# Two stacked mixers: block 1's feed-forward on rows without the norm's inverse

## The chip, the cores and the metric

One core of a Trainium2 chip runs the whole program. The metric is the device time of one execution in microseconds (us), the median of several runs.

## The reference

A first block of two layers and a second block of two layers run one after the other on the same 256 rows of 1024 values. The change is in the first block's second half, in both of its layers:

```
x = x + rms_norm(m, norm_mix_post[layer])          # m: output of the mixer
h = rms_norm(x, norm_ffn_pre[layer])
f = (silu(h @ w_gate) * (h @ w_up)) @ w_down       # 1024 -> 2816 -> 1024
x = x + rms_norm(f, norm_ffn_post[layer])

def rms_norm(x, w):
    return x * rsqrt(mean(x * x, -1) + 1e-6) * w
```

The norm's inverse root is one number for each token, so it can be applied to h or to the products of h.

## The kernel before

**Layout.** Activations lie with the features on the 128 partitions (eight tiles, k = 0 to 7) and the 256 tokens in the free dimension; xs holds x. Weights come from HBM as one stream of units of eight 128x128 blocks. One unit is one tile of 128 output columns in most products with 1024 rows. SyncE loads a unit into one of three raw buffers (L916), ScalarE rounds it to its high part w_hi (L1514), GpSimd computes the low part w_lo as the difference (L956, two instructions a unit); both are fp32r and have four slots. A raw buffer is free when the low part is done, a slot when TensorE has used the unit. Activations are split in high and low parts in the same way (hl). A product takes three partial products: in product_halves (L1014, L1018) one matmul of 512 columns multiplies the high weights with both halves of hl, one of 256 columns the low weights with the high half, and VectorE adds the two halves of the bank (add_halves, L2004).

**Order.** Every engine runs an order written out by hand, and waits on semaphores that count. Nothing reorders it. SyncE's loads are one list, weights and modulation units by the place of their use. The modulation units belong to block 2: its modulation vectors are computed in gaps of block 1, four fp32 matmuls a unit (modulation_unit, L1165), at named places; MID1 has six and PRE1 two. Behind some gates the finished rows are copied by VectorE (take_modulation, L2112, COPY zrow) and turned by TensorE (turn_modulation, L1176).

**The stretch.** After the output projection TensorE sums the squares of its result over the features, token by token (last_rows_sum, L1101), ScalarE takes the root, VectorE the reciprocal (L1966), and TensorE spreads the inverse over the partitions of a bank (spread_inverse, L1114). VectorE then forms the update (L2073) and adds it to xs (L2077), tile by tile; ScalarE squares the new tile (L1548); TensorE sums these squares (norm_sums), with the MID1 units between. A second root, reciprocal and spread follow, the PRE1 units run, and norm1 makes the rows: VectorE multiplies by weight and inverse (L1975), ScalarE rounds (L1579), VectorE subtracts (L1979). The first gate and up tiles run side by side on each k as it is ready (side_by_side, L1058 to L1061), the other 21 pairs tile by tile. VectorE adds the halves of gate and up, ScalarE applies SiLU (L1625) and rounds the hidden tile (L1770), VectorE multiplies (L2326) and makes the low part (L2320). The tiles ffg and ffu (gate, up) take banks 0, 1 and 3 in turn; bank 2 is STAT, bank 7 is X[4].

Of the kernel before, what the change touches and what calls it, by code (L numbers as in the profile page):

```python
# [12 lines left out]
P = 128  # L13
D = 1024
KD = D // P
# [459 lines left out]
SINGLE1, SINGLE2 = 1, 3  # L475


class Place:


    def __init__(self):
# [3 lines left out]
        for t in TILES:  # L485
            self.first_out.append(out)
            self.first_block.append(block)
            n = 1
            if t.wide == 2:
                n = 2 if t.array == "w_in" else T2 // P  # L490
            self.outs.append(n)
            pool = MANY if t.name in ("fa", "fg", "fd") or t.array == "w_out_2" else FEW
            if t.name in ("fa", "fg", "fd") and t.layer == DEPTH - 1:
                pool = THREE
            if t.array == "w_in" and t.name not in ("rg", "gr", "gate"):
                pool = WITH_STAT
            if t.array == "w_in_2" and t.name in ("ca", "cg"):
                pool = THREE
            if t.name in ("ffg", "ffu") or t.array in ("w_branch_a", "w_branch_b", "w_branch_c") or (t.array, t.name) == ("w_in", "gate"):
                pool = THREE  # L500
            for i in range(out, out + n):
                at = pool[(pool.index(self.bank[-1]) + 1) % len(pool)] if i and self.bank[-1] in pool else pool[0]
                self.bank.append(at)
# [54 lines left out]
def mixer_stack_kernel(nc, stream, vectors, consts, decay, gla_masks, positions, x_in, ctx_in, out):  # L558
# [201 lines left out]
    half_sum = STAT[:, 0:SEQ]  # L760


    def sem(name):
# [61 lines left out]
    merge_used, sum_ready, gate1_ready, ffg_ready = [  # L825
        sem(n) for n in ("merge_used", "sum_ready", "gate1_ready", "ffg_ready")]
# [74 lines left out]
    with nc.Block() as block:  # L901
# [66 lines left out]
        def _(pe):  # L968
# [149 lines left out]
            def last_rows_sum(c0, c1, single):  # L1118
# [7 lines left out]
                last.then_inc(stat_ready, 1)  # L1126
                spread_inverse(STAT, c0, c1)

# [59 lines left out]
            for l in range(DEPTH):  # L1188
# [312 lines left out]
        def _(act):  # L1501
# [118 lines left out]
            def on_sum(rows, func, scale, done):  # L1620
# [3 lines left out]
                act.wait_ge(tile_out, n + 1)  # L1624
# [18 lines left out]
            for l in range(DEPTH):  # L1643
# [119 lines left out]
                for t in range(NFF + 1):  # L1763
                    if t < NFF:
                        on_sum(ff_g[:, t % 2, :], ACT.Silu, 1.0, ffg_ready)
                        next_tile()
                        E.later(tile_done, 1)
                    if t:
                        E.need(ff_rows)
                        nc.scalar.activation(hid_hi[:, t - 1, :], half_sum, ACT.Copy).then_inc(ff_hi, 1)  # L1770
# [181 lines left out]
        def _(dve):  # L1952
# [98 lines left out]

            def add_normed(name, l):
# [17 lines left out]
                written = []  # L2070
                for k in range(KD + 1):
# [62 lines left out]
            for l in range(DEPTH):  # L2134
# [178 lines left out]
                dve.wait_ge(x_ready, KD * (2 * l + 1))  # L2313
                norm1("norm_ffn_pre", l)
                for t in range(NFF + 1):
                    if t < NFF:
                        add_halves(ff_g[:, t % 2, :])
# [3 lines left out]
                    if t < NFF:  # L2321
                        if t:
                            dve.wait_ge(ff_ready, NFF * l + t)
                        dve.wait_ge(tile_out, add_halves(half_sum))
                        E.need(ffg_ready)
# [355 lines left out]
```

## Time and profile before

| | us |
|---|---|
| median of 3 runs | 2690.48 (2689.98 to 2695.3) |
| the profiled execution's own time | 2693.33 |
| span of the profile | 2691.4 |
| granted TensorE clock, mean | 0.999 |
| busy: TensorE | 98% |
| busy: GpSimd, VectorE, ScalarE | 60%, 50%, 48% |
| median of the runs below the profiled execution's time | 2.85 |

The profile is of one execution, which took 2.85 us more than the median; its span is the part from the first to the last instruction. A share of busy time is a mean over stages; what the change touches is read from the stretch itself.

### The profile page before, as it was taken

The page shows a single profiled execution, that of the slowest core. Times are in us where ns is not written, and L with a number is a line of the kernel's source. Part 1 is how long each engine was busy: PE and PEld are TensorE (multiplying, and loading weights), DVE is VectorE, ACT ScalarE, POOL GpSimd, SP SyncE. Part 2 cuts the span into 40 slices and gives each one's busy share as a digit, 9 for nine tenths or more (in the row PEclk, how much of TensorE's full clock was granted, in tenths as well). Part 3 has the DMA queues.
Part 4 walks back from the last instruction along what each step waited for, and adds up shares of the span by engine and source line. Part 5 has one row for each costly group of instructions (what it writes and reads, how often), then busy time and mean ns, then how long its engine had stood idle before and what let it go on. Part 6 is the DMA issues. An engine that isn't in the chain of part 4 may idle for free.

```text
span 2691.4 us, 41592 instructions
## 1 busy us (share of the span) xinstructions
PE 2636.3 (98%) x16130; PEld 2260.6 (84%) x16130; DVE 1357.9 (50%) x2437; ACT 1283.0 (48%) x2042; POOL 1622.5 (60%) x1252
## 2 busy tenths in 40 slices
PE   8999999999999999999999999999999999999999
PEld 7998788899887888786788888888888889999888
DVE  6885533268654344875532434431333855335644
ACT  6464544455544454446433433442343565445654
POOL 6778688778786785432333345344443635458787
PEclk9999999999999999999999999999999999999999
DMA  6458676444787743221112122223222423234454
GB/s 216 141 182 283 228 255 226 160 139 154 253 274 236 248 167 124 84 74 56 63 63 87 63 88 101 87 94 102 94 94 79 142 86 118 95 110 157 166 187 165
DMA packets 145011, 386.12 MB, mean 143 GB/s; under 512 B 11968, under 2 KB 64448, under 8 KB 144832
## 3 DMA queue, kind: packets, MB, share of 16 engines
q1 hardware_dynamic: 144832, 383.61, 42.1%
q8 instruction: 128, 2.10, 0.3%
q14 instruction: 51, 0.42, 0.1%
HBM read 382.51 MB, written 1.05 MB: 143 GB/s over the span
## 4 chain that ended last, share of the span: by engine, by line
POOL 49%; issue 44%; PE 6%; POOLq 1%; DMA 0%; DVE 0%; ACT 0%; DVEq 0%; ACTq 0%
POOL w_lo L956 49%; PE bank L1014 4%; PE bank L1018 2%; POOLq L953 0%; DMA raw<-stream 0%; POOLq L960 0%; PE bank L1000 0%; PE bank L999 0%; PE bank L998 0%; ACT w_hi L1514 0%; DVE bank L2624 0%; ACT fc L1936 0%; DVE fc L2631 0%; DVE bank L2643 0%; POOLq L956 0%
## 5 line engine op out<-in xcount | busy, mean ns | idle before, releaser
L956 POOL TENSOR_TENSOR w_lo<-raw,w_hi 128x512 fp32r<-128x512 f32 x1248 | 1622.3, 1330 | 1060.4 <-ACT w_hi L1514 1057.7
L1514 ACT ACTIVATE w_hi<-raw 128x1024 fp32r<-128x1024 f32 x624 | 656.0, 1055 | 390.2 <-DMA raw<-stream 167.4
L998 PE MATMUL bank<-hl,w_hi 128*128 128x256 f32 (+1 forms) x2000 | 682.7, 341 | 1.9 <-POOL w_lo L956 1.0
L1000 PE MATMUL bank<-hl,w_lo 128*128 128x256 f32 (+1 forms) x2000 | 668.4, 334 | 0.0
L999 PE MATMUL bank<-hl,w_hi 128*128 128x256 f32 (+1 forms) x2000 | 668.3, 334 | 0.0
L998 PEld LDWEIGHTS bank<-hl,w_hi 128*128 128x128 f32 x2000 | 380.0, 190 | 45.7 <-issue 6.6
L999 PEld LDWEIGHTS bank<-hl,w_hi 128*128 128x128 f32 x2000 | 380.1, 190 | 41.0 <-issue 3.6
L1000 PEld LDWEIGHTS bank<-hl,w_lo 128*128 128x128 f32 x2000 | 379.8, 190 | 37.9
L1014 PE MATMUL bank<-hl,w_hi 128*128 128x512 f32 x1296 | 339.4, 395 | 2.8 <-POOL w_lo L956 2.5
L1014 PEld LDWEIGHTS bank<-hl,w_hi 128*128 128x128 f32 x1296 | 231.8, 189 | 50.4 <-issue 9.0
L1018 PEld LDWEIGHTS bank<-hl,w_lo 128*128 128x128 f32 x1296 | 178.9, 190 | 13.1
L1018 PE MATMUL bank<-hl,w_lo 128*128 128x256 f32 x1296 | 183.0, 282 | 0.0
L2631 DVE SCALAR_TENSOR_TENSOR fc<-bank,vec,fc 128x510 f32<-128x510 f32 (+1 forms) x88 | 54.2, 616 | 178.4 <-ACT fc L1936 178.4
L2361 DVE SCALAR_TENSOR_TENSOR xs<-bank,mod,xs 128x256 f32<-128x256 f32 x93 | 42.7, 481 | 177.5 <-PE bank L1000 132.8
L1014 PE MATMUL bank<-hid,w_hi 128*128 128x512 f32 x462 | 126.9, 394 | 0.0
L1936 ACT ACTIVATE fc<-bank,vec 128x512 f32<-128x512 f32 (+1 forms) x88 | 59.1, 672 | 141.9 <-PE bank L1000 108.8
L2416 DVE SCALAR_TENSOR_TENSOR bank<-z,vec,bank 128x512 f32<-128x512 f32 (+1 forms) x232 | 123.1, 617 | 0.0
L998 PE MATMUL bank<-y,w_hi 128*128 128x256 f32 (+1 forms) x336 | 110.6, 329 | 5.1 <-ACT gate L1537 4.4
L1081 PE MATMUL bank<-w_hi,hl 128*128 128x256 f32 x384 | 111.0, 289 | 2.0 <-POOL w_lo L956 1.4
L1000 PE MATMUL bank<-y,w_lo 128*128 128x256 f32 (+1 forms) x336 | 108.7, 324 | 0.0
L999 PE MATMUL bank<-y,w_hi 128*128 128x256 f32 (+1 forms) x336 | 108.6, 323 | 0.0
L1082 PE MATMUL bank<-w_lo,hl 128*128 128x256 f32 x384 | 108.6, 283 | 0.0
(330 smaller groups left out, 4066.4 us busy)
## 6 DMA issues: line engine op xcount, KB each, us to landing
raw<-stream SPq DMA_DIRECT2D x624, 512.0 KB, 3.3
spare_lo<-stream SPq DMA_DIRECT2D x32, 512.0 KB, 6.1
mix<-stream SPq DMA_DIRECT2D x32, 512.0 KB, 6.1
spare_hi<-stream SPq DMA_DIRECT2D x32, 512.0 KB, 5.8
xs<-x_rows SPq DMA_DIRECT2D x4, 256.0 KB, 4.1
xs<-ctx_rows SPq DMA_DIRECT2D x1, 1024.0 KB, 13.4
out_rows<-xs SPq DMA_DIRECT2D x8, 128.0 KB, 3.4
dec<-decay SPq DMA_DIRECT2D x1, 768.0 KB, 10.4
```

Source lines behind the costliest of these rows:

```text
L956: last = nc.gpsimd.tensor_tensor(w_lo[:, unit % SPLIT, part], raw[:, unit % RAW, part], w_hi[:, unit % SPLIT, part], ALU.subtract)
L998: nc.tensor.matmul(acc, wh, x[:, 0, k, c0:c1], start=k == 0, stop=False)
L999: nc.tensor.matmul(acc, wh, x[:, 1, k, c0:c1], start=False, stop=False)
L1000: last = nc.tensor.matmul(acc, wl, x[:, 0, k, c0:c1], start=False, stop=k == t.k - 1)
L1014: return nc.tensor.matmul(acc[:, :], w, x[:, :, k, c0:c1], start=k == 0, stop=k == t.k - 1)
L1018: return nc.tensor.matmul(acc[:, 0:SEQ], w, x[:, 0, k, c0:c1], start=False, stop=False)
L1081: nc.tensor.matmul(acc, h_hi[:, k, c:c + P], wh, start=k == 0, stop=False)
L1082: nc.tensor.matmul(acc, h_hi[:, k, c:c + P], wl, start=False, stop=False)
L1514: nc.scalar.activation(w_hi[:, n % SPLIT, :], raw[:, n % RAW, :], ACT.Copy).then_inc(hi_ready, 1)
L1936: nc.scalar.activation(fc[:, t % 2, j, cols], rows, ACT.Identity, bias=v_("ffn_conv_b_2", l, i), scale=v_("ffn_conv_w_2", l, 2 * NFF + i)) ...
L2416: C.do(V.scalar_tensor_tensor(out, z, w, y, MUL, ADD))
L2631: C.do(V.scalar_tensor_tensor(y[:, :, 1:], u[:, :, 0:SEQ - 1], w[0], y[:, :, 1:], MUL, ADD))
```

## The change

The rows of the feed-forward no longer contain the inverse: h is x times the weight, and every sum of the gate and up tiles is multiplied by the inverse, token by token, from a copy in sd, before SiLU or the product (add_scaled for the gate, a tensor_tensor for up). The sum of squares, the root and the spread of that inverse therefore run behind the first three tiles (gate, up, gate) instead of ahead of them: rows_before_norm takes each k of three tiles and then the sums of that k. The fourth tile gets a bank of its own, 5. One MID1 unit goes between the first sum and its spread, five follow the spread; the PRE1 units stand between the second sum and its spread. VectorE forms the update in bank 5, so that the addition to xs has one operand in PSUM. ScalarE makes the high part straight from xs with the weight as its scale, and rounds the fourth weight unit ahead of these rows, two more behind the second root, the others behind the first SiLU and the first hidden tile. The high part of a hidden tile now goes ahead of the next SiLU.

```diff
+    def update_row(k):
+        return banks[RAW_BANK][:, k % 2 * SEQ:(k % 2 + 1) * SEQ]
...
@@ TensorE
-                last_rows_sum(c0, c1, SINGLE1)
-                norm_sums(c0, c1, X[4], ADA_AT[l][MID1])
+                mid = ADA_AT[l][MID1]
+                last_rows_sum(c0, c1, SINGLE1, mid[:1])
+                rows_before_norm(hl, c0, c1, RAW_TILES, X[4], mid[1:])
                 modulation_at(l, PRE1)
-                for t in range(NFF):
-                    if t:
+                spread_inverse(X[4], c0, c1)
+                pe.wait_ge(ada_rows_out, MODS * l + 2)
+                product_halves(hl, c0, c1)
+                modulation_at(l, FFNS[0])
+                for t in range(1, NFF):
+                    if t > 1:
                         product_halves(hl, c0, c1, 2)
-                    else:
-                        side_by_side(hl, c0, c1, 2, h_ready, halves=True)
                     modulation_at(l, FFNS[t])
...
+            def rows_before_norm(x, c0, c1, count, bank, units):
...
+                for k in range(KD):
+                    E.need(h_ready)
+                    for i, acc in enumerate(accs):
...
+                        last = nc.tensor.matmul(acc[:, :], wh, x[:, :, k, c0:c1], start=k == 0, stop=k == KD - 1)
...
+                    E.need(sq_ready)
+                    last = token_sums(bank, work[:, k, :], c0, c1, k == 0, k == KD - 1)
...
@@ ScalarE
-                squares_of_x(c0, c1)
+                split_freed()
+                for k in range(KD):
+                    E.need(x_ready)
+                    nc.scalar.activation(h_hi[:, k, c0:c1], xs[:, k, c0:c1], ACT.Copy,
+                                         scale=v_("norm_ffn_pre", l, k)).then_inc(hi_done, 1)
+                    square(k, xs, c0, c1, sq_ready)
                 token_roots(X[4], c0, c1)
-                split_norm(c0, c1)
...
@@ VectorE
+            def add_scaled(dst):
+                n = E.later(tile_out, 1) - 1
+                dve.wait_ge(tile_done, n + 1)
+                V.reduce_sum(gate_sum, both_halves(banks[PLACE.bank[n]]), AX_X).then_inc(tile_out, 1)
+                dve.wait_ge(tile_out, n + 1)
+                V.tensor_tensor(dst, gate_sum, sd[:, 0:SEQ], MUL).then_inc(ffg_scaled, 1)
...
+                    for k in range(KD + 1):
+                        if k < KD:
+                            C.do(V.scalar_tensor_tensor(update_row(k), mix[:, k, c0:c1], v_(name, l, k),
+                                                        STAT[:, c0:c1], MUL, MUL))
+                        if k:
+                            E.need(hi_done)
+                            V.scalar_tensor_tensor(h_lo[:, k - 1, c0:c1], xs[:, k - 1, c0:c1],
+                                                   v_("norm_ffn_pre", l, k - 1), h_hi[:, k - 1, c0:c1], MUL, SUB)\
+                                .then_inc(h_ready, 1)
+                        if k < KD:
+                            C.settle()
+                            V.tensor_tensor(xs[:, k, c0:c1], update_row(k), xs[:, k, c0:c1], ADD).then_inc(x_ready, 1)
+                    token_inverses(c0, c1)
+                    C.do(V.tensor_copy(sd[:, 0:SEQ], X[4][:, c0:c1]))
...
-                norm1("norm_ffn_pre", l)
                 for t in range(NFF + 1):
-                    if t < NFF:
-                        add_halves(ff_g[:, t % 2, :])
                     if t:
                         dve.wait_ge(ff_hi, NFF * l + t)
                         V.tensor_tensor(hid_lo[:, t - 1, :], half_sum, hid_hi[:, t - 1, :], SUB).then_inc(ff_ready, 1)
                     if t < NFF:
+                        add_scaled(ff_g[:, t % 2, :])
...
                         dve.wait_ge(tile_out, add_halves(half_sum))
+                        C.do(V.tensor_tensor(half_sum, half_sum, sd[:, 0:SEQ], MUL))
+                        C.settle()
                         E.need(ffg_ready)
                         V.tensor_tensor(half_sum, ff_g[:, t % 2, :], half_sum, MUL).then_inc(ff_rows, 1)
```

TensorE in layer 0, from the first sum to the first tiles, before (the numbers ahead of the rows are places in its order; silu_c rows are modulation units, four matmuls each, cst,work rows are sums, cst,sd rows spreads):

```order
1491 L1101 MATMUL bank<-cst,work 128x128 x4
1492 L1114 MATMUL bank<-cst,sd 128x128 x2
1493 L1165 MATMUL bank<-spare_hi,silu_c 2x256 x8
1494 L1165 MATMUL bank<-spare_lo,silu_c 2x256 x4
1495 L1101 MATMUL bank<-cst,work 128x128 x4
1496 L1165 MATMUL bank<-spare_lo,silu_c 2x256 x4
...
1501 L1101 MATMUL bank<-cst,work 128x128 x4
1502 L1114 MATMUL bank<-cst,sd 128x128 x2
1503 L1165 MATMUL bank<-spare_hi,silu_c 2x256 x8
1504 L1059 MATMUL bank<-hl,w_hi 128x512
```

And now, the same place:

```order
1491 L1110 MATMUL bank<-cst,work 128x128 x4
1492 L1201 MATMUL bank<-spare_hi,silu_c 2x256 x4
1493 L1123 MATMUL bank<-cst,sd 128x128 x2
1494 L1201 MATMUL bank<-spare_hi,silu_c 2x256 x4
1495 L1201 MATMUL bank<-spare_lo,silu_c 2x256 x8
1496 L1201 MATMUL bank<-mix,silu_c 2x256 x8
...
1504 L1154 MATMUL bank<-hl,w_lo 128x256
1505 L1155 MATMUL bank<-hl,w_hi 128x512
...
1509 L1155 MATMUL bank<-hl,w_hi 128x512
1510 L1110 MATMUL bank<-cst,work 128x128 x2
```

The sums of the second norm, which stood together between the units, now stand one k at a time behind six matmuls of three tiles.

VectorE at the start of the feed-forward's tiles, before (ff_g is the gate tile's sum, zrow the copy of the modulation rows):

```order
238 L1979 TENSOR_TENSOR hl<-work,hl 128x256 x3
239 L2004 TENSOR_REDUCE ff_g<-bank 128x256
240 L2004 TENSOR_REDUCE bank<-bank 128x256
241 L2326 TENSOR_TENSOR bank<-ff_g,bank 128x256
242 L2112 COPY zrow<-bank 128x256
```

And now:

```order
236 L2022 RECIPROCAL sd<-sd 128x2
237 L2148 COPY sd<-bank 128x256
238 L2111 TENSOR_REDUCE bank<-bank 128x256
239 L2113 TENSOR_TENSOR ff_g<-bank,sd 128x256
240 L2060 TENSOR_REDUCE bank<-bank 128x256
241 L2403 TENSOR_TENSOR bank<-bank,sd 128x256
242 L2406 TENSOR_TENSOR bank<-ff_g,bank 128x256
243 L2192 COPY zrow<-bank 128x256
244 L2396 TENSOR_TENSOR hid<-bank,hid 128x256
```

The copy of the modulation rows stands behind six instructions that wait for the second spread.

## Rows read from the trace of the kernel before

**Rows 1.** The page: busy time of TensorE; the rounding of weights by ScalarE.

```profile
PE 2636.3 (98%) x16130; PEld 2260.6 (84%) x16130; DVE 1357.9 (50%) x2437; ACT 1283.0 (48%) x2042; POOL 1622.5 (60%) x1252
...
L1514 ACT ACTIVATE w_hi<-raw 128x1024 fp32r<-128x1024 f32 x624 | 656.0, 1055 | 390.2 <-DMA raw<-stream 167.4
```

**Rows 2.** Timeline, TensorE, layer 0's stretch and layer 1's start: start, us, engine, instruction.

```profile
305.48 1.35 PE L1101 MATMUL bank<-cst,work 128*128 128x128 f32 x8
...
307.38 0.71 PE L1114 MATMUL bank<-cst,sd 128*128 128x128 f32 x4 [0.55 <-DVE sd L1966]
...
308.02 1.04 PE L1165 MATMUL bank<-spare_hi,silu_c 128*2 128x256 f32 x16
...
308.89 0.61 PE L1165 MATMUL bank<-spare_lo,silu_c 128*2 128x256 f32 x8
...
311.21 0.61 PE L1165 MATMUL bank<-spare_lo,silu_c 128*2 128x256 f32 x8
...
311.76 1.16 PE L1101 MATMUL bank<-cst,work 128*128 128x128 f32 x8
...
312.85 0.61 PE L1165 MATMUL bank<-mix,silu_c 128*2 128x256 f32 x8
...
316.80 0.71 PE L1114 MATMUL bank<-cst,sd 128*128 128x128 f32 x4 [0.62 <-DVE sd L1966]
...
815.22 1.35 PE L1101 MATMUL bank<-cst,work 128*128 128x128 f32 x8
```

**Rows 3.** Timeline, TensorE, first tiles, turned rows, and fp32r behind a unit.

```profile
319.41 0.47 PE L1059 MATMUL bank<-hl,w_hi 128*128 128x512 f32 x1 [0.92 <-DVE hl L1979]
...
325.11 0.40 PE L1014 MATMUL bank<-hl,w_hi 128*128 128x512 f32 x1
...
330.70 0.38 PE L1176 MATMUL bank<-cst,zrow 128*128 128x128 f32 x2
...
330.84 0.48 PE L1014 MATMUL bank<-hl,w_hi 128*128 128x512 f32 x1
...
344.03 0.50 PE L1014 MATMUL bank<-hl,w_hi 128*128 128x512 f32 x1
...
344.37 0.88 PE L1018 MATMUL bank<-hl,w_lo 128*128 128x256 f32 x6
```

**Rows 4.** Timeline, VectorE and ScalarE, the update and the first extraction.

```profile
308.13 0.87 DVE L2073 SCALAR_TENSOR_TENSOR work<-mix,vec,bank 128x256 f32<-128x256 f32 x2 [0.80 <-PE bank L1114]
...
309.26 0.48 DVE L2073 SCALAR_TENSOR_TENSOR work<-mix,vec,bank 128x256 f32<-128x256 f32 x1
...
309.38 0.42 ACT L1548 ACTIVATE work<-xs 128x256 f32<-128x256 f32 x1 [2.24 <-DVE xs L2077]
...
323.88 1.28 ACT L1625 ACT_TABLE_LOAD   x1
...
325.56 0.69 DVE L2004 TENSOR_REDUCE bank<-bank 128x256 f32<-128x512 f32 x1
...
326.28 0.43 DVE L2326 TENSOR_TENSOR bank<-ff_g,bank 128x256 f32<-128x256 f32 x1
...
326.62 0.42 DVE L2112 COPY zrow<-bank 128x256 f32<-128x256 f32 x1
```

**Rows 5.** Lines L2275 and L2320: duration ns min/median/max, first and last start.

```profile
L2275 DVE SCALAR_TENSOR_TENSOR y<-mix,y x16: 411/720/1416, 256.8 to 794.6; 128x256 fp32r<-128x256 f32 x16
...
L2320 DVE TENSOR_TENSOR hid<-bank,hid x44: 424/425/426, 331.1 to 965.2; 128x256 fp32r<-128x256 f32 x44
```

**Rows 6.** Timeline, GpSimd, first unit behind the stretch.

```profile
323.94 2.53 POOL L956 TENSOR_TENSOR w_lo<-raw,w_hi 128x512 fp32r<-128x512 f32 x2 [15.37 <-ACT w_hi L1514]
```

**Rows 7.** Timeline of SyncE; loads from 344 and from 317 us: KB, median us to landing.

```profile
318.12 1.29 SPq L925 DMA_DIRECT2D spare_hi<-stream  x2
...
raw<-stream SPq DMA_DIRECT2D x5, 512.0 KB, 4.8
...
spare_hi<-stream SPq DMA_DIRECT2D x2, 512.0 KB, 7.4
```

More of the change, by code:

```diff
@@ L475 @@
 SINGLE1, SINGLE2 = 1, 3
+RAW_TILES, RAW_BANK = 3, 5
+RAW_LAST = [[t for t in TILES if t.name in ("ffg", "ffu") and t.layer == l][RAW_TILES] for l in range(DEPTH)]
 class Place:
@@ L502, in __init__ @@
                 at = pool[(pool.index(self.bank[-1]) + 1) % len(pool)] if i and self.bank[-1] in pool else pool[0]
+                if t is RAW_LAST[t.layer]:
+                    at = RAW_BANK
                 self.bank.append(at)
@@ L1126, in last_rows_sum @@
                 last.then_inc(stat_ready, 1)
+                for unit in units:
+                    modulation_unit(unit)
                 spread_inverse(STAT, c0, c1)
+            def rows_before_norm(x, c0, c1, count, bank, units):
+                first = at["tile"]
+                accs = [bank_of(PLACE.first_out[first + i]) for i in range(count)]
+                stat_free()
+                for unit in units:
+                    modulation_unit(unit)
+                for k in range(KD):
+                    E.need(h_ready)
+                    for i, acc in enumerate(accs):
+                        u = PLACE.first_block[first + i] // UNIT
+                        wait_unit(u)
+                        wh, wl = w_hi[:, u % SPLIT, k * P:(k + 1) * P], w_lo[:, u % SPLIT, k * P:(k + 1) * P]
+                        if k:
+                            nc.tensor.matmul(acc[:, 0:SEQ], wl, x[:, 0, k, c0:c1], start=False, stop=False)
+                        last = nc.tensor.matmul(acc[:, :], wh, x[:, :, k, c0:c1], start=k == 0, stop=k == KD - 1)
+                        if k == 0:
+                            last = nc.tensor.matmul(acc[:, 0:SEQ], wl, x[:, 0, k, c0:c1], start=False, stop=False)
+                        if k == KD - 1:
+                            last.then_inc(tile_done, 1)
+                    E.need(sq_ready)
+                    last = token_sums(bank, work[:, k, :], c0, c1, k == 0, k == KD - 1)
+                last.then_inc(stat_ready, 1)
+                at["tile"] += count
             def norm_sums(c0, c1, bank, units=(), spread_bank=None, spare=0):
@@ L1618, in square_rows, with on_sum @@
                 nc.scalar.activation(mix[:, KD - 1, c0:c1], last, ACT.Copy).then_inc(tile_out, 1)
-            def on_sum(rows, func, scale, done):
+            def on_sum(rows, func, scale, done, before=None):
                 n = next_tile()
                 E.later(tile_done, 1)
-                act.wait_ge(tile_out, n + 1)
+                if before:
+                    before()
+                    E.need(ffg_scaled)
+                else:
+                    act.wait_ge(tile_out, n + 1)
                 nc.scalar.activation(rows, rows, func, scale=scale).then_inc(done, 1)
@@ L1759, in _, with hidden_high @@
                 token_roots(STAT, c0, c1)
-                squares_of_x(c0, c1)
-                token_roots(X[4], c0, c1)
-                split_norm(c0, c1)
-                for t in range(NFF + 1):
-                    if t < NFF:
[L1765 to L1768, printed above, removed]
-                        E.need(ff_rows)
-                        nc.scalar.activation(hid_hi[:, t - 1, :], half_sum, ACT.Copy).then_inc(ff_hi, 1)
+                split_freed()
[4 more added lines that the diff above has]
+                    square(k, xs, c0, c1, sq_ready)
+                token_roots(X[4], c0, c1)
+                ahead = at["unit"] + 1
+                split_through(ahead)
+                def hidden_high(t):
+                    if t >= 0:
+                        E.need(ff_rows)
+                        nc.scalar.activation(hid_hi[:, t, :], half_sum, ACT.Copy).then_inc(ff_hi, 1)
+                    if t == 0:
+                        split_through(ahead + 2)
+                for t in range(NFF):
+                    on_sum(ff_g[:, t % 2, :], ACT.Silu, 1.0, ffg_ready, lambda: hidden_high(t - 1))
+                    if t == 0:
+                        split_through(ahead + 1)
+                    next_tile()
+                    E.later(tile_done, 1)
+                hidden_high(NFF - 1)
                 square_rows(l == DEPTH - 1)
```

15 lines of the change are left out of this document (9 added, 6 removed).

## The prediction

> **What bounds the kernel now.** I read the page's busy times first: TensorE is busy for 98% of the span [rows 1], so time can be gained only where TensorE stands idle, and work moved off other engines is worth nothing. Then the timeline of TensorE around the place that the diff touches, which is the stretch between block 1's output projection and its feed-forward, once per layer. In layer 0 it begins at 305.48 us (the first matmul of the sum of squares) and reaches the feed-forward's fifth tile, the third gate, at 330.84 [rows 2, 3], 25.36 us later. Layer 1 runs through the same rows from 815.22 [rows 2]. I call 305.48 the origin and count from it.
>
> The reader is to see how full that stretch already is. Its named waits are 0.55 us for the first reciprocal, 0.62 for the second and 0.92 for the first normalised rows [rows 2, 3]. Its work up to the end of the two tiles side by side (325.11, 19.63 us from the origin) is: first sum 1.1, two spreads of 0.64, eight modulation units 4.0, the sums of eight rows 4.4, sixteen pairs of matmuls 5.6, together 16.4 by the prices below. So about 3.2 us per layer are idle, 6.4 in both, 0.24% of the run, and that is the most that the change can bring. In the feed-forward behind it the rows follow one another without a wait.
>
> **The change part by part, for one layer.** All is counted from the origin on TensorE.
>
> *First sum and spread.* The sum is unchanged, 1.35 us with its wait. One modulation unit now stands between it and the spread; two in a row take 0.87 (308.02 to 308.89), a lone one among other matmuls 0.55 (311.21 to 311.76) [rows 2]. It ends at +1.90, and the reciprocal was there before +1.90 too, so the unit is free: spread from +1.92, 0.64 long (307.38 to 308.02), to +2.56. Five units follow: 5 times 0.435 and 0.1 for the switch, 2.28, to +4.84.
>
> *Raw rows, eight steps.* Each step is six matmuls of three tiles and two sums. Sixteen pairs of the two side by side tiles took 5.70 (319.41 to 325.11) [rows 3], 0.35 us each behind the first; three are 1.05. The sums of two steps take 1.09 (311.76 to 312.85), so one 0.545. Together 1.60, or 12.8 us for eight. But the step changes between the two kinds of matmul twice. The first fp32r matmul after fp32 ones holds TensorE 0.34 us (344.03 to 344.37) [rows 3] (a whole pair takes 0.35, and this is its longer half, so some 0.1 of it is the switch), and a lone spread of two matmuls takes 0.64 where two such of a row take 0.545. No row shows this alternation, so its cost is bounded: from 0 to 0.25 a step, and I take 0.17, near the sum of the two differences. Eight steps of 1.77: 14.2 (12.8 to 14.8).
>
> Is TensorE the pace there? The first row needs: spread to VectorE 0.75 (307.38 to 308.13), update 0.48 and add 0.42 (0.43 with a PSUM input), ScalarE 0.42, low part 0.48, and handovers of 0.05 each [rows 2, 4]: +4.6, ahead of +4.84. Each further step is add, ScalarE, low part and handovers, 0.42 + 0.42 + 0.48 + 0.15, about 1.5 (1.3 where the update's issue overlaps), under 1.77. The squares come behind the high part, 0.84 of ScalarE a step, under it too.
>
> *A shared port.* GpSimd now rounds the fourth unit at once, some 308.6 to 311.1, since ScalarE takes it behind the first root (1.05 us [rows 1], while VectorE waits for the spread); in the kernel before, GpSimd stood idle for 15.37 us here [rows 6]. While GpSimd is busy, a VectorE instruction with two SBUF inputs varies: the like of the new low part in the merge took 0.41 to 1.42 us, median 0.72, the one with a PSUM input 0.42 to 0.43 always [rows 5]. The update and its add have a PSUM input; the low part has two SBUF inputs. The first one starts at about +4.1 and may end anywhere from +4.6 to +5.5; I take 0.2 us of TensorE's time, 0 to 0.7. The Trainium skill states in GPSIMD Engine Reference, Key points: GpSimd shares its SBUF interfaces with VectorE and contends with instructions with two SBUF inputs. The trace agrees, with 0.42 against 0.72; by the rule the edit pays up to 0.7 us a layer, without it nothing.
>
> So the eight steps end at 4.84 + 0.2 + 14.2 = +19.24, with three tiles done.
>
> *Second sum, spread and fourth tile.* Two PRE1 units, 0.98, cover the root and the reciprocal (for which TensorE waited 0.62 with nothing between). They end at +20.2. The spread, 0.64, then the fourth tile, eight pairs or 2.80, end at +23.65. In the kernel before the fourth tile ended at about +25.2 (330.70), so the raw rows are worth 1.5 us here.
>
> *A new wait.* Behind the fourth tile TensorE turns the modulation rows (330.70 in [rows 3]), and needs the copy of them by VectorE, which stands behind the first gated product. Before, that copy ran at 326.62, 4 us early [rows 4]. Now all extraction of tiles starts behind the second spread: 0.75 from the spread's start, copy of the inverse 0.42, reduce 0.69, scaling 0.43, reduce 0.69, scaling 0.43, product 0.43, copy of the rows 0.42 [rows 4], less some overlap of issue, with handovers of 0.04: about 4.3 us. From +20.2 that is +24.5, and TensorE, ready at +23.65, waits 0.9 us. The SiLU doesn't add to it: its scaled rows are there 2.4 us after the spread's start, and the table load (1.28) [rows 4], behind the rounding of two units, is over by about 1.8. The two transposes, 0.14, end at +24.7, where the fifth tile starts. Before: +25.36. **Gain 0.66 us per layer.**
>
> *Weights.* At +24.7 units five and six must be rounded. ScalarE starts five 0.3 us after the eight steps, GpSimd takes 2.53 a unit [rows 6]: ready 3.0 us behind the PRE1 units, needed at 4.5. Unit seven's load stands in SyncE's queue behind the eight modulation loads, the last two of which wait for the PRE1 units; it leaves 0.9 us after them (the like two were issued from 318.12 to 319.41) [rows 7]. With modulation loads beside it a weight load landed in 4.8 us, two modulation loads together in 7.4 [rows 7]. With 4.8: 5.7, high part 1.06 [rows 1], low part 2.53, 9.3 us behind the PRE1 units, needed at 10.1 (4.5 and two tiles of 2.80). Hidden by 0.8. Unit eight follows at GpSimd's 2.53 against 2.80.
>
> *Per tile pair* VectorE gets two scalings more, 0.86 us. Its chain in a pair (low part, two reduces, two scalings, product, handovers) is some 3.7 of 5.6 us, and SiLU's lateness of 0.9 leaves the rounding of weights ahead: hidden. At the end the last hidden row is 0.45 later, needed 7.4 us into the down projection: hidden. The fourth tile's own bank keeps it from waiting for the first extraction. TensorE's matmuls are the same in number.
>
> **Sum.** 2 layers of 0.66 are 1.3 us: the profiled execution would have a span of 2690.1 instead of 2691.4, and its own time 2692.0 instead of 2693.3. The median of the runs, 2690.48, lies 2.85 below that time; the same step gives 2689.2. Bounds: with 12.8 for the steps and no contention the gain is 2.2 per layer; with 14.8 and 0.7 it is -0.4.
>
> **Rivals.**
> 1. *Clean interleave*: switching costs nothing. Gain 2.2 per layer, 2686.1. For it: a switch from fp32r to fp32 shows no gap in [rows 3]. Against: the 0.34 us the other way.
> 2. *VectorE and ScalarE set the pace of the eight steps* (slower). Each step is a round trip of three dependent instructions, with two SBUF inputs in one. From 1.85 us a step the gain is gone; at 2.1 a layer loses 2.0, and the time is 2694.5. Against: the parts sum to 1.5.
> 3. *Unit seven late* (slower). If its load behind two modulation loads lands in their 7.4 us, its low part is ready 11.9 behind the PRE1 units against 10.1 needed: 1.9 us per layer lost, net 1.2, the time 2693.0. From 5.6 us of landing on it costs.
> 4. *The change doesn't do what it says*: waits only move (a second wait on the extraction chain), 2690.5.
>
> **How the numbers follow.** The forecast has 0.60, rivals 1 to 4 have 0.12, 0.10, 0.10 and 0.08. Predicted 2689.2. The forecast alone spans 2686.5 to 2691.3; the range 2685.8 to 2693.0 takes in rivals 1, 3 and 4. A measurement of this kernel can tell a change from about 0.2%, 5.4 us. Faster by more needs nearly the whole idle time, 0.04; slower by more needs 2.7 a layer, the tail of rival 2 or 2 and 3 together, 0.07; within it 0.89.
>
> **What would show it.** On TensorE: eight steps of 1.77 us from about 4.9 us after the first sum; the transposes after the fourth tile waiting 0.9 us for VectorE's copy; no wait for a low part at the seventh tile; the fifth tile 24.7 us after the origin. On VectorE low parts of 0.48 but for the first or second. A step over 1.85, with TensorE waiting for VectorE's low part, shows rival 2; a wait for GpSimd at the seventh tile rival 3; steps of 1.6 rival 1. Wrong altogether would be a change of time outside this stretch.

## The result and the profile after

The changed kernel takes 2700.86 us (median of 13 runs, 2696.33 to 2707.41) against 2693.25 for the kernel before (13 runs): ratio 1.0027, with a 95% interval of 1.002 to 1.0035. It is slower by 7.6 us; the prediction had 1.3 us faster and 2693.0 as the upper end of its range. The profiled execution of the changed kernel took 2707.41 us, with a span of 2705.6, 6.5 above its own median. So I compare lengths of stretches within the traces and leave the rest of that execution alone. A second profile of the same kernel (below) took 2701.32.

The stretch runs from the first matmul of the sum of squares to the first matmul of the down projection, once per layer:

| kernel | layer 0, us | layer 1, us |
|---|---|---|
| before | 145.8 | 148.1 |
| after | 149.0 | 153.9 |
| after, second profile | 147.4 | 153.2 |

The second profile is longer by 1.6 and 5.1, together 6.7, where its medians differ by 6.9 (2701.32 against 2694.46). Outside these two stretches the same two traces differ by 1.4 us in sum: single parts by -1.1 to +2.5, and the largest part (from the sum of squares behind layer 1's down projection to the end) takes 1662.5 to 1667.8 us over the fourteen profiles of this text, with no order by kernel. So I look for the loss in the two stretches; the experiments, which take it away there, bear that out. The page after, for [rows 1]:

```profile
PE 2640.9 (98%) x16130; PEld 2265.0 (84%) x16130; DVE 1394.7 (52%) x2511; ACT 1285.8 (48%) x2042; POOL 1619.7 (60%) x1252
```

TensorE has the same 16130 matmul records, yet is busy 4.6 us longer. The timeline of TensorE after (start, us, instruction, idle time before it and what ended it), layer 0 with origin 306.90, then two rows of layer 1; it answers to [rows 2, 3]:

```profile
306.90 1.35 PE L1110 MATMUL bank<-cst,work 128*128 128x128 f32 x8
...
308.80 0.71 PE L1123 MATMUL bank<-cst,sd 128*128 128x128 f32 x4
...
312.55 0.50 PE L1155 MATMUL bank<-hl,w_hi 128*128 128x512 f32 x1 [0.78 <-DVE hl L2141]
...
313.72 0.60 PE L1110 MATMUL bank<-cst,work 128*128 128x128 f32 x4
314.08 0.36 PE L1154 MATMUL bank<-hl,w_lo 128*128 128x256 f32 x1
...
315.22 0.61 PE L1110 MATMUL bank<-cst,work 128*128 128x128 f32 x4
...
324.73 1.05 PE L1201 MATMUL bank<-spare_hi,silu_c 128*2 128x256 f32 x16
325.71 0.71 PE L1123 MATMUL bank<-cst,sd 128*128 128x128 f32 x4
326.18 0.47 PE L1023 MATMUL bank<-hl,w_hi 128*128 128x512 f32 x1
...
330.00 0.44 PE L1212 MATMUL bank<-cst,zrow 128*128 128x128 f32 x2 [0.78 <-DVE zrow L2192]
330.19 0.48 PE L1023 MATMUL bank<-hl,w_hi 128*128 128x512 f32 x1
...
336.76 0.79 PE L1023 MATMUL bank<-hl,w_hi 128*128 128x512 f32 x1 [3.52 <-DVE bank L2111]
337.35 1.91 PE L1027 MATMUL bank<-hl,w_lo 128*128 128x256 f32 x8
339.05 2.49 PE L1023 MATMUL bank<-hl,w_hi 128*128 128x512 f32 x8
...
844.74 0.44 PE L1212 MATMUL bank<-cst,zrow 128*128 128x128 f32 x2 [0.77 <-DVE zrow L2192]
850.90 0.80 PE L1023 MATMUL bank<-hl,w_hi 128*128 128x512 f32 x1 [5.72 <-DVE bank L2111]
```

A row merges several records, and an fp32 matmul leaves two: the four records of the row at 313.72 are the two matmuls of one sum.

Up to the fifth tile the change works better than forecast: it starts at 330.19, 23.29 us from the origin, where the kernel before had 25.36. Then comes a wait that the kernel before doesn't have: 3.52 us ahead of the sixth tile in layer 0, 5.72 ahead of the fifth in layer 1. It is for the reduce at L2111, which reads an earlier tile out of the bank that the new tile wants. What was late is in the timelines of the other engines, layer 0; it answers to [rows 4, 6, 7]:

```profile
308.46 3.75 POOL L965 TENSOR_TENSOR w_lo<-raw,w_hi 128x512 fp32r<-128x512 f32 x3
...
311.07 1.43 DVE L2141 SCALAR_TENSOR_TENSOR hl<-xs,vec,hl 128x256 fp32r<-128x256 f32 x1 [0.18 <-ACT hl L1806]
...
325.41 1.21 SPq L934 DMA_DIRECT2D spare_hi<-stream  x2
...
326.67 4.83 SPq L925 DMA_DIRECT2D raw<-stream  x3
...
334.31 1.06 ACT L1553 ACTIVATE w_hi<-raw 128x1024 fp32r<-128x1024 f32 x1 [5.58 <-DMA raw<-stream]
335.27 0.36 ACT L1816 ACTIVATE hid<-bank 128x256 fp32r<-128x256 f32 x1
...
335.67 0.42 DVE L2396 TENSOR_TENSOR hid<-bank,hid 128x256 fp32r<-128x256 f32 x1 [5.73 <-ACT hid L1816]
336.01 0.69 DVE L2111 TENSOR_REDUCE bank<-bank 128x256 f32<-128x512 f32 x1
...
841.41 13.51 SPq L925 DMA_DIRECT2D raw<-stream  x5
...
848.45 1.06 ACT L1553 ACTIVATE w_hi<-raw 128x1024 fp32r<-128x1024 f32 x1 [4.98 <-DMA raw<-stream]
```

Read it backwards. The sixth tile (336.76) waits for the reduce of 336.01. VectorE runs it behind the low part of the first hidden row (335.67), which waited 5.73 us for ScalarE's high part (335.27). ScalarE's order has that high part behind the rounding of unit seven (334.31), which waited 5.58 us for its load. That load was issued at 326.67, behind two modulation loads: 7.6 us of landing and start. In layer 1 it was issued at 841.41 and rounded at 848.45, 7.0 us.

One link of this chain is new and easy to overlook. The diff puts VectorE's reduce of the next gate tile behind the low part of the hidden row; in the kernel before it stood ahead of it, and so the third tile's bank was read out while the hidden row was still awaited:

```profile
328.10 0.69 DVE L2004 TENSOR_REDUCE ff_g<-bank 128x256 f32<-128x512 f32 x1 [1.07 <-PE bank L1014]
331.15 0.42 DVE L2320 TENSOR_TENSOR hid<-bank,hid 128x256 fp32r<-128x256 f32 x1 [2.35 <-ACT hid L1770]
```

No run puts the reduce back ahead, so what that alone would do isn't shown.

Behind the wait the granted clock is lower (stretches of time: length, busy us of PE, PEld, DVE, ACT and POOL, granted clock, DMA share, GB/s):

```profile
334.00:338.00 4.00, 1.24 (x5) 1.15 (x6) 2.26 (x5) 2.73 (x4) 2.56 (x3) 0.84 0.24 93
338.00:342.00 4.00, 4.00 (x20) 3.56 (x20) 2.70 (x6) 1.71 (x4) 2.42 (x2) 0.74 0.49 164
...
850.00:854.00 4.00, 3.10 (x11) 2.88 (x12) 3.16 (x7) 1.58 (x3) 4.00 (x4) 0.50 0.24 70
```

A granted clock of 0.50 is the lower level, 1.2 GHz of 2.4; 0.74 is a mix of both. Eight low part matmuls take 1.91 us there (337.35) and 1.12 elsewhere.

**The account.** Layer 0: 2.07 us gained up to the fifth tile, 3.52 of wait, and 4.62 us for the sixth tile and the first matmul of the seventh (336.76 to 341.38) where the same matmuls usually take 3.1 (330.19 to 330.50, then 2.80 for a tile), so 1.5 to the clock: +3.0, measured +3.2. Layer 1 in the same way: -2.2, +5.7 and +2.1, so +5.6, measured +5.9.

### The profile page after: what moved, and what is told of

It is laid out like the page before. It is cut to its first block, busy times and chain, and to the rows that moved or that the text cites. A ratio compares the mean times of both kernels' runs of the same rounds, so it can differ in the third digit from the quotient of the medians.

```text
span 2705.6 us, 41665 instructions
## 1 busy us (share of the span) xinstructions
PE 2640.9 (98%) x16130; PEld 2265.0 (84%) x16130; DVE 1394.7 (52%) x2511; ACT 1285.8 (48%) x2042; POOL 1619.7 (60%) x1252
## 4 chain that ended last, share of the span: by engine, by line
POOL 52%; issue 46%; PE 1%; POOLq 1%; DVE 0%; DMA 0%; ACT 0%; DVEq 0%; ACTq 0%
POOL w_lo L965 52%; PE bank L1023 1%; POOLq L962 0%; PE bank L1027 0%; POOLq L969 0%; DMA raw<-stream 0%; DVE fc L2711 0%; ACT fc L1992 0%; PE bank L1009 0%; PE bank L1008 0%; PE bank L1007 0%; ACT w_hi L1553 0%; DVE bank L2723 0%; POOLq L965 0%; DVE bank L2704 0%
```

## The experiments

Each batch ran beside the kernel before on the same chip, so each total is a ratio to that. "Stretch" is the one of the table above.

### Batch one: the chain behind the wait

My theory A: the late load of unit seven, through ScalarE's order and the bank, makes the wait, and the wait makes the lower clock. Theory B puts the loss elsewhere.

**The first hidden row ahead of the rounding of unit seven.**

```diff
                     if t >= 0:
                         E.need(ff_rows)
                         nc.scalar.activation(hid_hi[:, t, :], half_sum, ACT.Copy).then_inc(ff_hi, 1)
                     if t == 0:
+                        split_through(ahead + 1)
                         split_through(ahead + 2)
...
-                    if t == 0:
-                        split_through(ahead + 1)
```

> The changed kernel, but ScalarE makes the first hidden tile's high part ahead of the rounding of the seventh weight unit instead of behind it. Theory A (ScalarE's order: it stands 5 to 5.6 us before the late load of unit seven, and so keeps back the first hidden tile, VectorE's third-tile extraction, and the bank of TensorE's sixth tile): TensorE's wait for VectorE's reduce at the sixth tile (3.5 and 5.7 us) goes, and what is late next is unit seven itself, at the seventh tile, for some 2 us a layer; together 3 to 6 us faster than the changed kernel. Rival B (the bank is late for another reason, such as VectorE's two scalings more per pair): the wait at the sixth tile stays above 2.5 us and the time is that of the changed kernel.

Measured: ratio 0.999 (0.9981 to 0.9999); stretches 144.4 and 146.9, so 4.7 and 7.1 us less than after. The load is still late (ScalarE waits for it, 2.97 us in the row below), but the bank is no longer behind it. ScalarE's timeline, layer 0:

```profile
327.55 0.38 ACT L1816 ACTIVATE hid<-bank 128x256 fp32r<-128x256 f32 x1 [0.92 <-DVE bank L2405]
330.91 1.06 ACT L1553 ACTIVATE w_hi<-raw 128x1024 fp32r<-128x1024 f32 x1 [2.97 <-DMA raw<-stream]
```

Behind the turned rows TensorE keeps 0.8 us for a low part of GpSimd in layer 0 and 0.7 for the bank in layer 1. One moved instruction on ScalarE removes the loss. It gains more than A forecast: the ratio falls by 0.0037, some 10 us, against 3 to 6, because the 2 us expected at the seventh tile came as 0.8 in one layer alone and the lower clock went with the wait.

**The loads of weights ahead of the modulation loads.**

```diff
-            order.append((used[i - ADA_SLOTS] if i >= ADA_SLOTS else first, 1, l * ADA_LAYER + i))
+            behind_pre1 = i >= ADA_SLOTS and l * ADA_LAYER + i - ADA_SLOTS in ADA_AT[l][PRE1]
+            order.append((used[i - ADA_SLOTS] + behind_pre1 if i >= ADA_SLOTS else first, 1, l * ADA_LAYER + i))
```

> The changed kernel, but in SyncE's list the load of the seventh weight unit stands ahead of the two modulation loads that wait for the PRE1 units instead of behind them. Theory A (the load's place in the queue is the root of the loss): it is issued some 13 us earlier, ScalarE doesn't wait 5 us for it, TensorE's wait at the sixth tile goes, and so does the drop of its clock; both stretches end 2 us a layer earlier than in the kernel before, the whole is 6 to 10 us faster than the changed kernel, that is 2 to 4 us below the kernel before. Rival B (three weight loads and two modulation loads share the DMA engines, whatever their order): unit eight is late instead, TensorE waits 2 us or more within the sixth to ninth tile, and at most half of that is gained.

Measured: ratio 0.9989 (0.9979 to 1.0); stretches 143.1 and 147.0, 2.7 and 1.1 under the kernel before. The load was issued 10.1 and 9.4 us behind the first sum instead of 19.8 and 19.6, so some 10 us earlier and not 13. Its issue and its rounding in layer 0 (first sum at 306.77), and the DMA view of it (KB, us to landing):

```profile
316.89 1.30 SPq L926 DMA_DIRECT2D raw<-stream  x1
327.86 1.04 ACT L1554 ACTIVATE w_hi<-raw 128x1024 fp32r<-128x1024 f32 x1
raw<-stream SPq DMA_DIRECT2D x1, 512.0 KB, 8.3
```

It took even longer to land than in the kernel after, 8.3 us against 7.6 (8.7 against 7.0 in layer 1), and was still there before ScalarE wanted it: the rounding at 327.86 has no wait. So it is the place in the queue that counts, not the speed of the load. Rival B is right about unit eight, for which ScalarE now waits 2.42 us, but TensorE doesn't wait for it.

Both ends of the chain, the load and ScalarE's order, are thus shown each by its own edit. The Trainium skill, in DMA: Bandwidth & Descriptors, section Issuing engines are not separate DMA queues, says that DMAs run on the same 16 DMA engines and interleave, whichever engine issued them. All loads here are issued by SyncE, so no run shows the second half; the first fits the 8.3 us of this load, issued behind six modulation loads, where the median weight load of the same profile landed in 3.4.

**Both edits.**

> Both edits together. Theory A: the same as the load ahead alone within 1 us, since one of them already takes the wait away. Rival B (the order on ScalarE costs also with the load in time): another 1 us or more.

Measured: ratio 0.9979 (0.997 to 0.9988); stretches 143.1 and 147.1, the same as with the load alone within 0.1, as A says. The two totals differ by 0.001, which their intervals don't separate. Once the load is in time the second edit has nothing to remove.

**The copy of the modulation rows ahead of the tiles**, on top of both.

```diff
                 add_normed("norm_mix_post", l)
+                modulation_at(l, FFNS[0])
                 for t in range(NFF + 1):
...
-                        modulation_at(l, FFNS[t])
+                        if t:
+                            modulation_at(l, FFNS[t])
```

> Both edits, and VectorE copies the modulation rows ahead of the extraction of the first tiles. Theory: the wait of 0.78 us at the turned rows goes in both layers, 1.5 us in all, and nothing else moves. Rival: the extraction, 0.35 us later, makes a bank late, and the wait moves to the fifth or sixth tile.

Measured: ratio 0.9987 (0.9978 to 0.9995); stretches 142.0 and 148.7. Layer 0 gains 1.1 (0.2 of it the wait of the first row, which isn't there in this profile) and TensorE waits for nothing there. In layer 1 the rival holds: it loses 1.6, since TensorE comes 0.8 earlier to a bank that isn't free, and the copy of 0.42 stands ahead of the reduce that frees it. TensorE in layer 1:

```profile
834.61 0.38 PE L1213 MATMUL bank<-cst,zrow 128*128 128x128 f32 x2
837.01 0.50 PE L1024 MATMUL bank<-hl,w_hi 128*128 128x512 f32 x1 [2.02 <-DVE bank L2111]
837.35 1.19 PE L1028 MATMUL bank<-hl,w_lo 128*128 128x256 f32 x8
838.33 3.54 PE L1024 MATMUL bank<-hl,w_hi 128*128 128x512 f32 x8
```

The last row takes 2.00 us elsewhere. A wait of 0.8 was removed, one of 0.7 became 2.0, and the clock took the rest.

### Batch two: banks, clock, port

**Banks in turn past the fourth tile's.** With the fourth tile in bank 5, after's rotation begins again at bank 0. Tiles one to seven have 3, 0, 1, 5, 0, 1, 3 in layer 0 and 1, 3, 0, 5, 0, 1, 3 in layer 1. So the sixth tile (layer 0) or the fifth (layer 1) takes the bank of the third, whose extraction is the late one. This edit, on the kernel after, gives 3, 0, 1, 5, 3, 0, 1.

```diff
-                at = pool[(pool.index(self.bank[-1]) + 1) % len(pool)] if i and self.bank[-1] in pool else pool[0]
+                prev = self.bank[-1 - (self.bank[-1] == RAW_BANK and pool is THREE)] if i else None
+                at = pool[(pool.index(prev) + 1) % len(pool)] if prev in pool else pool[0]
```

> The changed kernel, but behind the fourth tile the three banks go on in turn from the third tile's bank instead of starting again at bank 0, so that tiles five, six and seven take the banks of tiles one, two and three in both layers (in the changed kernel tile three's bank came to tile six in layer 0 and to tile five in layer 1). Theory A (the loss is the late extraction of tile three, met at the tile that takes its bank): TensorE's waits at tiles six and five go, and the next to wait is tile seven in both layers, for the same extraction or for its own low part, behind the late load: 1 to 2.5 us each; the changed kernel's time less 4 to 6 us. Rival B (the banks don't matter, the load is late for all): the waits keep their 3.5 and 5.7 us.

Measured: ratio 0.9994 (0.9983 to 1.0004), some 9 us under the kernel after where 4 to 6 were expected; stretches 144.6 and 146.6, less than after by 4.5 and 7.3. The waits of 3.5 and 5.7 are gone; what is left by name behind the first row is 0.7 and 0.4 for GpSimd, under the 1 to 2.5 of A, and the 0.8 for the copy. From 334 to 338 TensorE stands 0.73 us idle where it had stood for 2.76, and the clock stays whole:

```profile
334.00:338.00 4.00, 3.27 (x18) 2.56 (x18) 3.45 (x8) 1.63 (x3) 4.00 (x4) 1.00 0.29 84
338.00:342.00 4.00, 4.00 (x23) 3.24 (x21) 2.86 (x8) 2.58 (x4) 2.37 (x3) 1.00 0.64 208
```

The load is still late here, so the bank is the third link that breaks the chain alone.

**All four edits.**

> All four edits: the load of unit seven ahead, the hidden tile's high part ahead, the copy of the modulation rows ahead, and the banks in turn. Theory: TensorE waits nowhere between the first row and the down projection in either layer; both stretches from the first sum to the down projection are 3.5 us shorter than in the kernel before (142.0 and some 144.3 us against 145.8 and 148.1), the time 7 us below it, 0.26%. Rival (the pace of weights sets the stage once TensorE doesn't wait for banks): waits for GpSimd's low parts of 1 us or more within the first ten tiles.

Measured: 2689.42 us, ratio 0.9974 (0.9965 to 0.9984); stretches 142.2 and 144.7, that is 3.6 and 3.4 under the kernel before. TensorE's only named waits are 0.3 and 0.4 us for the first rows. This version beats both kernels, by 0.26% against the one before.

**Throwaway matmuls in the waits**, on the kernel after, to hold the clock up.

```diff
-                    if t > 1:
+                    if t == 2:
+                        if l:
+                            keep_busy(X[3], 13)
+                        product_halves(hl, c0, c1)
+                        if not l:
+                            keep_busy(X[3], 8)
+                        product_halves(hl, c0, c1)
+                    elif t > 2:
```

> The changed kernel, with matmuls of no use in the place of TensorE's long wait: 8 ahead of the sixth tile in layer 0, 13 ahead of the fifth in layer 1. Theory A (idle TensorE also lost its clock, so that the two tiles behind the wait ran at a lower granted clock and took 6.5 to 7.5 us instead of 5.6): the granted clock stays 1.00, each stretch is 1 to 2 us shorter than in the changed kernel, though TensorE has more to do. Rival B (the lower clock is not a result of the wait): the clock falls there all the same and nothing is gained.

Measured: ratio 1.0038 (1.0026 to 1.005); stretches 147.0 and 150.8. The clock is 1.00 in all windows from 328 to 344 and from 836 to 852, and the tiles behind run at 1.12 and 2.00 us, so the lower clock was the consequence of TensorE's idle time. The stretches are 2.0 and 3.1 shorter than in the first profile of after. But the total isn't below after's, against A. The trace shows 67.4 us from the down projection to the next sum in layer 1, where after has 63.5. Batch three follows that.

**The update through SBUF instead of PSUM**, on top of all four.

```diff
-        return banks[RAW_BANK][:, k % 2 * SEQ:(k % 2 + 1) * SEQ]
+        return work[:, k, SEQ:T2]
```

> The kernel with all four edits, but VectorE's update of x goes through SBUF, as in the kernel before, instead of through PSUM. Theory A (a VectorE instruction with two SBUF inputs is slow while GpSimd rounds): the first addition to x takes 1 us or more instead of 0.42, the first row comes 0.5 to 1.5 us later, and each layer loses as much. Rival B (only the low part is hit): the additions take 0.42 us and the time is the same.

Measured: ratio 0.9976 (0.9965 to 0.9988), no difference in the total; stretches 143.4 and 145.4, 1.2 and 0.7 more. The add's line with PSUM, then with SBUF (ns min/median/max), and the two slow ones in the timeline:

```profile
L2147 DVE TENSOR_TENSOR xs<-bank,xs x16: 408/418/424, 311.5 to 828.3; 128x256 f32<-128x256 f32 x16
```

```profile
L2147 DVE TENSOR_TENSOR xs<-work,xs x16: 413/419/1503, 310.5 to 830.3; 128x256 f32<-128x256 f32 x16
...
312.54 1.50 DVE L2147 TENSOR_TENSOR xs<-work,xs 128x256 f32<-128x256 f32 x1
...
819.17 1.44 DVE L2147 TENSOR_TENSOR xs<-work,xs 128x256 f32<-128x256 f32 x1
```

One add in each layer is slow: the first in layer 1, the second in layer 0, whose first took 0.71. TensorE waits 0.47 and once more 0.73 us in layer 0 and 1.19 in layer 1, against 0.27 and 0.44 through PSUM. So A is seen in the rows, and in this pair of profiles the way through PSUM is worth about a microsecond a layer; the total can't show that much.

### Batch three: is the wait there every time, and what eats the filler's gain

**The changed kernel again.**

> The changed kernel once more, with no edit, beside the three below; its first profiled execution had taken 2707.4 us, 6.5 above its own median. A (the waits of 3.5 and 5.7 us are part of the program): both come again within 0.5 us, with the granted clock under 0.9 behind them, and the stretches from the first sum to the down projection are 149 and 154 us again, within 1.5. B (they belong to one execution, with late transfers): at least one stretch is under 146 or 150. The ratio by A is 1.002 to 1.0035; the total of the profiled execution is nearer to 2701.

Measured: 2701.32 us, ratio 1.0025 (1.0016 to 1.0034); stretches 147.4 and 153.2. TensorE, and a window behind the first of the two waits:

```profile
333.00 0.50 PE L1023 MATMUL bank<-hl,w_hi 128*128 128x512 f32 x1 [2.22 <-DVE bank L2111]
...
845.70 0.80 PE L1023 MATMUL bank<-hl,w_hi 128*128 128x512 f32 x1 [5.44 <-DVE bank L2111]
```

```profile
334.00:338.00 4.00, 4.00 (x16) 3.35 (x15) 2.60 (x7) 1.47 (x3) 2.67 (x3) 0.60 0.56 153
```

Both waits come again. The one of layer 0 is 1.3 us shorter, more than the 0.5 that A allowed, and its load, issued at 324.21 and rounded at 330.55, took 6.3 us instead of 7.6: the wait follows the landing one for one. The stretch of layer 0 is under A's 149 by 1.6, just outside. So the size of the wait in layer 0 differs between executions, and its presence doesn't. A third profile without an edit of layer 0 (below, filler in layer 1 alone) fits too: a load of 6.0 us and a wait of 1.9.

**The filler again, and in one layer at a time.**

> The changed kernel with throwaway matmuls in both waits, once more (16 single matmuls in layer 0, 26 in layer 1). Its first profile had a new wait of 2.3 us for GpSimd's low part at 997.9 in layer 1's down projection, with a clock of 0.54 behind it, and took 3.9 us there. A (that wait is a chance of the stream of weights in that execution): the stretch from the down projection to the next sum is 63.5 us here, the total some 4 to 5 us under the changed kernel's. B (the filler causes it, since layer 1's tensor work now reaches the down projection 3 us earlier, while weights come no earlier): 67 us again, and the total is not below the changed kernel's by more than 2 us.

With only the line `keep_busy(X[3], 8)` left in:

> Throwaway matmuls in layer 0's wait alone. A and B of the run with both: layer 0's stretch 147.0 us, layer 1's 153.9, the down projection behind it 63.5; the total about 2 us under the changed kernel's. If the down projection takes 67 here too, the filler in layer 1 isn't its cause.

With only `keep_busy(X[3], 13)`:

> Throwaway matmuls in layer 1's wait alone. Layer 0's stretch 149.0 us, layer 1's 150.8. A: the down projection behind it 63.5 and the total about 3 us under the changed kernel's. B: 67 and the total within 1 us of the changed kernel's.

Measured, of all profiles:

| filler in | layer 0 stretch | layer 1 stretch | down projection to next sum, layer 1 | ratio |
|---|---|---|---|---|
| none | 149.0, 147.4 | 153.9, 153.2 | 63.5, 63.5 | 1.0027, 1.0025 |
| both | 147.0, 147.3 | 150.8, 151.1 | 67.4, 67.8 | 1.0038, 1.0033 |
| layer 0 | 146.8 | 153.1 | 64.8 | 1.0031 |
| layer 1 | 146.0 | 151.6 | 64.9 | 1.0031 |

In layer 1 the filler saves 2.2 us (mean 151.2 against 153.4). By chance unit seven also landed 0.3 us sooner in the filled profiles (mean 6.3 against 6.6), so the clock's share of the loss is 1.9 to 2.2. In layer 0 nothing can be resolved against the spread of the load; the last row, which has no filler in layer 0, is the shortest (its wait was 1.9 us, with a clock of 1.00 in all windows from 330 to 342). With both, 4.1 us are given back in the down projection, in both profiles: B, and not chance. No single filler gave B's 67 or A's 63.5, and none lowered the total, where every A had it 2 to 5 us lower. TensorE's waits for low parts in that part follow its length: 0.7 us with no filler, 2.0 and 1.8 with one, 3.0 and 3.2 with both. How: in the second filled run VectorE, ScalarE, GpSimd and TensorE of that place show

```profile
988.23 1.32 DVE L2079 TENSOR_SCALAR half_w<-vec 128x8 f32<-128x8 f32 x1
989.46 1.34 DVE L2078 TENSOR_SCALAR half_b<-vec 128x24 f32<-128x24 f32 x1
...
993.16 0.84 ACT L1658 ACTIVATE hl<-bank,mod 128x256 fp32r<-128x256 f32 x2 [5.39 <-DVE bank L2112]
993.89 2.95 ACT L1560 ACTIVATE w_hi<-raw 128x1024 fp32r<-128x1024 f32 x3
...
995.02 8.71 POOL L965 TENSOR_TENSOR w_lo<-raw,w_hi 128x512 fp32r<-128x512 f32 x7 [4.25 <-ACT w_hi L1560]
...
997.57 1.93 PE L1027 MATMUL bank<-hid,w_lo 128*128 128x256 f32 x8 [2.31 <-POOL w_lo L965]
```

and the kernel after, for the same two instructions of VectorE:

```profile
995.51 0.16 DVE L2072 TENSOR_SCALAR half_w<-vec 128x8 f32<-128x8 f32 x1
995.58 0.17 DVE L2071 TENSOR_SCALAR half_b<-vec 128x24 f32<-128x24 f32 x1
```

Two of four tiny instructions took 1.3 us each instead of 0.16, in both filled profiles and in those with one filler (1.27 or 1.28 there). In after, GpSimd stood idle at that moment (from 995.47 to 996.38); in the second filled run it made low parts of weights (975.65 to 990.77). VectorE's chain came later, ScalarE stood 5.4 us on its result with three units to round queued behind, and TensorE ran out of rounded weights: a wait of 2.3 us, and again a lower clock behind it (0.63 from 999 to 1002). The tiny instructions are a part of this at most, since they were as slow with one filler, where the down projection took 64.8 and 64.9. It is the same shape as the loss of the change: a wait on ScalarE's order turns into one of weights. The Trainium skill, in GPSIMD Engine Reference, section Key points, says that GpSimd contends with VectorE's instructions in a 2-port mode or with two SBUF inputs. The trace agrees in so far as they were slow only while GpSimd worked, 1.32 against 0.16, though two of the four took 0.16 or 0.17 then too; these have one tensor from SBUF, and no row shows their mode. Why both fillers together cost more than the sum of single ones stays open.

## Why the prediction was wrong, point by point

- **First sum, spread, five units**: right. The units end 4.87 us from the origin (312.55 less its wait), against 4.84.
- **The shared port**: 0.2 was taken of a range of 0 to 0.7. It measured 0.78 and 0.64 in the first profile, with the first low part at 1.43 us. The upper end was the better guess: the edit itself puts GpSimd's work (308.46 to 312.21) over that moment. Over all profiles through PSUM the wait of the first row lies between 0 and 0.9.
- **Eight steps**: 14.2 (12.8 to 14.8) was forecast, 12.18 measured (312.55 to 324.73), 1.50 a step. A sum (four records) takes 0.36 (313.72 to 314.08), not 0.545, and six matmuls behind it 1.14 (314.08 to 315.22), 0.09 above three pairs. By this split the alternation costs 0.09, not 0.17, and the sum was overpriced by half, as it was priced at half of a group of eight records. Rival 2 falls: no step waits. Rival 1 came nearer than the forecast, with its 1.6 a step and 2.2 a layer against 1.50 and 2.07 measured; its time was undone behind the fifth tile. With sums that cheap, the 3.2 us a layer that I called the most the change can bring weren't the most either: the version with all four edits gains 3.6 and 3.4.
- **PRE1 units, spread, fourth tile**: the units start 1.4 us early (17.83 against 19.24), by the two terms above. The matmul behind the spread came at 0.47, not 0.64.
- **The new wait for the copy**: 0.9 forecast, 0.78 and 0.77 measured, and the edit that removes it gains 1.1 us in layer 0. Its chain, forecast at 4.3 us from the spread, took 4.29 (325.71 to 330.00). The fifth tile came at 23.29, not 24.7: gain 2.07 where 0.66 was forecast.
- **Weights, the step that failed.** "Hidden by 0.8" rested on a landing of 4.8 us, the median of five loads elsewhere. The issue came as forecast (0.96 us behind the PRE1 units, against 0.9), the landing took 7.6 and 7.0. Rival 3 named this lateness and its threshold of 5.6, but priced it by the wrong queue: GpSimd's low part at the seventh tile, 1.9 us. Its sum is right for the path that it follows: with the hidden row out of the way, a load of 6.3 us in layer 0 made a wait of 0.79 there, where the sum gives 0.7. But the load's first user is ScalarE, and the high part of the first hidden row stands behind it there, VectorE's reduce of the third tile behind that, and TensorE's sixth or fifth tile behind its bank: 3.5 and 5.7 us. I had asked who needs the rounded unit, not what is queued behind its rounding. Rival 4 named a second wait on the extraction chain, but let it cost no more than the change gains.
- **"The fourth tile's own bank keeps it from waiting"**: true of the fourth, and it moved the wait. Taking the fourth out of the rotation gave the third tile's bank to the sixth or fifth. In the kernel before, the rotation had no such jump, and the reduce of the third tile stood ahead of the hidden row's low part. I hadn't followed the banks of the tiles behind.
- **The clock** had no term at all. The waits brought it down, 1.5 us in layer 0 and 2.1 in layer 1 by the rows, 1.9 to 2.2 by the filler in layer 1.
- **Per tile, VectorE's two scalings**: hidden, as forecast. With all four edits no wait is left in the tiles.

## What to carry to other kernels

When a load may be late, look for every instruction that stands behind its first user on that engine, and follow each to TensorE; the price is the longest of these paths, not the one of the data. When a tile is taken out of a rotation of banks, write down the banks of the next three and compare them with the tiles whose extraction the change delays. A new wait on TensorE can cost more than its length: here the matmuls behind waits of 3.5 and 5.7 us ran at a lower clock, for 1.5 and 2.1 us more.

## What the runs showed of the hardware that I had not expected

- TensorE's granted clock was lower behind waits of 5.7 (0.50), 3.5 (0.74), 2.2 (0.60) and 2.0 us (0.79), and full behind one of 1.9 us and behind those of 0.8. Throwaway matmuls in the first two kept it whole.
- A VectorE instruction on 128x8 values took 1.32 us while GpSimd was at work, its like 2.5 us later only 0.16; both took 0.16 where GpSimd stood idle.
- A weight load of 512 KB landed in 3.2 us at the median of the kernel after, in 7.6 and 7.0 right behind two modulation loads, and in 8.3 and 8.7 when it was issued earlier, behind the other six.
- Two fp32 matmuls (four records) between fp32r ones let the next one start after 0.36 us, where four in a group had taken 1.09.
